# RWKV outputs of a two-block network: sums by accumulating transfers and head-by-head ScalarE steps for eight of ten tiles

## The reference, cut to what matters

```
rw_l = rw_l_f + flip_t(rw_l_b)
rw_c = rw_c_f + flip_t(rw_c_b)
...
mean = jnp.mean(rw_y, axis=-1, keepdims=True)
var = jnp.mean(jnp.square(rw_y - mean), axis=-1, keepdims=True)
gn = ((rw_y - mean) * lax.rsqrt(var + RWKV_GN_EPS)).reshape(bl, l, RWKV_W) * rw_ln_w + rw_ln_b
bonus = sum(jnp.sum(r * dirs[d][1] * rw_rk, axis=-1, keepdims=True) * v for d in range(2))
rw_o = (gn + bonus.reshape(bl, l, RWKV_W)) * jax.nn.silu(u[..., E_WZ:E_SHIFT])
```

## Time and profile before

| | |
|---|---|
| median of 3 runs | 4666.36 us (4665.85 to 4668.23) |
| profiled execution, its own time | 4666.31 us |
| span in the profile | 4664.5 us |
| PE busy | 4091.0 us (88%) |
| PE weight loads busy | 3356.1 us (72%) |
| DVE busy | 2628.1 us (56%) |
| ACT busy | 1482.7 us (32%) |
| POOL busy | 648.3 us (14%) |
| RWKV stage | about 2865 to 3500 us of the span |

### The profile page before, as it was taken

One profiled execution on the slowest core, in us unless ns is written; L12 is line 12 of the kernel. 1 busy time (PEld: TensorE's weight loads), 2 busy tenths in 40 slices (PEclk: granted clock), 3 DMA queues, 4 the chain that ended last, 5 costly groups with the idle time before them and its releaser, 6 DMA issues. The chain is left out here.

```text
span 4664.5 us, 74388 instructions
## 1 busy us (share of the span) xinstructions
PE 4091.0 (88%) x28926; PEld 3356.1 (72%) x28926; DVE 2628.1 (56%) x5018; ACT 1482.7 (32%) x3133; POOL 648.3 (14%) x860
## 2 busy tenths in 40 slices
PE   6999998867999989699996586899868899989988
PEld 5998887556888877599986233787757789955646
DVE  4567774666334348611227586777765335565746
ACT  4233321744222235311004243334434311143432
POOL 1111111000000000011123112000010024333320
PEclk8999999888999999799997688999878999999989
DMA  5544442542111145422323485444434335453334
GB/s 194 172 150 145 146 136 84 186 154 89 47 45 46 35 145 162 128 87 86 119 100 106 148 307 207 112 117 133 118 91 151 125 118 187 155 156 102 97 106 141
DMA packets 429678, 598.68 MB, mean 128 GB/s; under 512 B 168495, under 2 KB 317443, under 8 KB 426725
## 3 DMA queue, kind: packets, MB, share of 16 engines
q1 hardware_dynamic: 377069, 417.99, 29.6%
q0 software_dynamic: 50192, 173.75, 10.0%
q10 hardware_dynamic: 2088, 2.49, 0.2%
HBM read 429.40 MB, written 164.71 MB: 127 GB/s over the span
## 5 line engine op out<-in xcount | busy, mean ns | idle before, releaser
L612 PE MATMUL g_in_g_acc<-g_in_g_whi,g_in_hi 128*128 128x444 f32 (+4 forms) x960 | 357.2, 372 | 15.3 <-DVE g_in_g_wlo L600 10.3
L613 PE MATMUL g_in_g_acc<-g_in_g_wlo,g_in_hi 128*128 128x444 f32 (+4 forms) x960 | 346.4, 361 | 0.0
L614 PE MATMUL g_in_g_acc<-g_in_g_whi,g_in_lo 128*128 128x444 f32 (+4 forms) x960 | 345.7, 360 | 0.0
L612 PE MATMUL g_even_g_acc<-g_even_g_whi,h_hi 128*128 128x428 f32 (+2 forms) x800 | 289.8, 362 | 11.8 <-DVE g_even_g_wlo L600 11.8
L613 PE MATMUL g_even_g_acc<-g_even_g_wlo,h_hi 128*128 128x428 f32 (+2 forms) x800 | 289.3, 362 | 0.0
L614 PE MATMUL g_even_g_acc<-g_even_g_whi,h_lo 128*128 128x428 f32 (+2 forms) x800 | 289.3, 362 | 0.0
L612 PE MATMUL g_odd_g_acc<-g_odd_g_whi,h_hi 128*128 128x344 f32 (+3 forms) x816 | 263.7, 323 | 24.7 <-DVE g_odd_g_o L632 14.4
L5223 DVE SCALAR_TENSOR_TENSOR up_cv<-up_acc,up_taps,up_cv 128x1023 f32<-128x1023 f32 x88 | 112.8, 1282 | 281.4 <-ACT up_cv L5199 274.1
L614 PE MATMUL g_odd_g_acc<-g_odd_g_whi,h_lo 128*128 128x344 f32 (+3 forms) x816 | 262.0, 321 | 0.0
L613 PE MATMUL g_odd_g_acc<-g_odd_g_wlo,h_hi 128*128 128x344 f32 (+3 forms) x816 | 261.4, 320 | 0.0
L5178 PE MATMUL up_acc<-h_hi,up_w_hi 128*128 128x512 f32 x704 | 220.3, 395 | 8.7 <-DVE up_w_lo L5216 8.7
(11 more groups left out here) (585 smaller groups left out, 9741.4 us busy)
## 6 DMA issues: line engine op xcount, KB each, us to landing
down_raw<-in_w_down SPq DMA_DIRECT2D x66, 512.0 KB
g_in_m_w<-in_ada_w SPq DMA_DIRECT2D x24, 1024.0 KB, 5.6
up_w_buf<-in_w_up SPq DMA_DIRECT2D x44, 512.0 KB
g_odd_x<-U3p SPq DMA_DIRECT2D x24, 768.0 KB, 6.8
g_in_m_w<-in_w_ada SPq DMA_DIRECT2D x16, 1024.0 KB, 5.9
prep_near<-U2q SPq DMA_DIRECT2D x18, 896.0 KB
PD<-prep_od POOLq DMA_DIRECT2D x10, 1536.0 KB, 9.0
rwkv_xd<-PD SPq DMA_DIRECT2D x20, 768.0 KB
```

The lines of the kernel that those rows point to most:

```text
L612: pe.matmul(bank[:, :wd], hi[:, k, tt], w_hi[:, st % 2, k, :wd], start=k == 0, stop=False)
L613: pe.matmul(bank[:, :wd], hi[:, k, tt], w_lo[:, st % 2, k, :wd], start=False, stop=False)
L614: op = pe.matmul(bank[:, :wd], lo[:, k, tt], w_hi[:, st % 2, k, :wd], start=False, stop=k == KC - 1)
```

## The change

For outputs 0 to 7:

- The second direction is no longer loaded into `yo` and added by DVE. SP loads `RW[0]` into `yx` (new semaphore `y_half`), and a new POOL step `y_sum` waits for it and issues a transfer that adds `RW[1]` into `yx` (`accum_op`).
- `y_square` is eight activations of 64 columns, one for each head, with `accum_out` to `yvars`; the DVE sum of the squares goes away.
- The bonus leaves POOL: a new ACT step `y_gain`, between `y_silu` and `y_root`, multiplies v by the head's number in eight activations of 64 columns, scaled by a column of `ydots`. Then `s.y_bonus` rises.
- The row `rw_ln_b` is added into `yv` by a new POOL step `y_bias`, a second accumulating transfer with the row broadcast over partitions. `y_end` waits for its landing (`y_biased`).

Outputs 8 and 9 keep their code; their bonus on POOL signals `y_bonus_late`. `y_load_z` of 8 and 9 still waits for `s.y_bonus >= n - 1`. The first, replaced copies of the functions are gone from the file too; the instructions of all other stages stand as before.

```diff
-              ... ("T2_out", -1), ("y_silu", 1), ("y_root", 1), ("turn0", 2), ...
+              ... ("T2_out", -1), ("y_silu", 1), ("y_gain", 1), ("y_root", 1), ("turn0", 2), ...
-              ... ("y_scale", 1), ("X1", 0),
+              ... ("y_scale", 1), ("y_bias", 1), ("X1", 0), ("y_sum", 0),
...
-             ("y_silu", K8 - 1), ("y_root", K8 - 1), ("y_scale", K8 - 1), ("y_end", K8 - 1), ("u", END), ("u_out", END),
+             ("y_silu", K8 - 1), ("y_gain", K8 - 1), ("y_bias", K8 - 1), ("y_root", K8 - 1), ("y_scale", K8 - 1), ("y_end", K8 - 1), ("u", END), ("u_out", END),
...
-                    got = own_in[n] if n >= K8 else s.y_in
...
-                    sp.dma_start(yx[:, d], RW[0, tile, :]).then_inc(got, DMA)
-                    sp.dma_start(other_in(n), RW[1, tile, :]).then_inc(got, DMA)
+                    if n >= K8:
+                        sp.dma_start(yx[:, d], RW[0, tile, :]).then_inc(own_in[n], DMA)
+                        sp.dma_start(other_in(n), RW[1, tile, :]).then_inc(own_in[n], DMA)
+                    else:
+                        sp.dma_start(yx[:, d], RW[0, tile, :]).then_inc(s.y_half, DMA)
...
+                if what == "y_sum":
+                    pool.wait_ge(s.y_half, (n + 1) * DMA)
+                    pool.dma_start(yx[:, d], RW[1, i * P:(i + 1) * P, :], accum_op=ALU.add).then_inc(s.y_in, DMA)
+                if what == "y_bias":
+                    pool.wait_ge(s.y_bonus, n + 1)
+                    pool.dma_start(yv[:].rearrange("p h d -> p (h d)"), ln_b.partition_broadcast(P), accum_op=ALU.add).then_inc(s.y_biased, DMA)
-                if what == "y_bonus":
+                if what == "y_bonus" and n >= K8:
...
-                    act.activation(by_head(other_in(n)), yx[:, d].rearrange("p (h d) -> p h d", d=HD), ACT.Square).then_inc(s.y_squared, 1)
+                    if n >= K8:
+                        act.activation(by_head(other_in(n)), yx[:, d].rearrange("p (h d) -> p h d", d=HD), ACT.Square).then_inc(s.y_squared, 1)
+                    else:
+                        for h in range(HN):
+                            act.activation(yo[:, h * HD:(h + 1) * HD], yx[:, d, h * HD:(h + 1) * HD], ACT.Square, accum_out=yvars[:, d, h])
+                        act.drain()
+                        act.sem_inc(s.y_squared, 1)
+                if what == "y_gain":
+                    act.wait_ge(s.y_in_z, (n + 1) * (3 * DMA))
+                    for h in range(HN):
+                        act.activation(yv[:, h], yv[:, h], ACT.Copy, scale=ydots[:, d, h])
+                    act.drain()
+                    act.sem_inc(s.y_bonus, 1)
```

More of the change, by code:

```diff
@@ L29 @@
-ALPHA = 2.0 ** 0.25
-DMA = 16
-@contextmanager
-def stage(nc, name, *signals):
-    sems = {s: nc.alloc_semaphore(f"{name}_{s}") for s in signals}
-    with ExitStack() as mem:
-        def sb(label, shape, dt=F32):
-            return mem.enter_context(nc.sbuf_tensor(f"{name}_{label}", shape, dt))
-        def ps(label, shape=(P, 512), dt=F32):
-            return mem.enter_context(nc.psum_tensor(f"{name}_{label}", list(shape), dt))
-        with nc.Block() as block:
-            yield block, namedtuple("Signals", signals)(**sems), sb, ps
-    nc.clear_and_free_semaphores(list(sems.values()))
-    nc.all_engine_barrier()
@@ L3332, in part @@
                     pool.drain()
-                    pool.sem_inc(s.y_bonus, 1)
+                    pool.sem_inc(s.y_bonus_late, 1)
                 if what == "y_end":
@@ L3635, in part @@
                         dve.wait_ge(own_in[n], 2 * DMA)
[L3636 to L3639 removed]
+                        dve.tensor_tensor(yn, yn, other_in(n), ALU.add)
+                        dve.drain()
+                    else:
+                        dve.wait_ge(s.y_in, (n + 1) * DMA)
                     dve.tensor_reduce(ymean[:, :, 0], yn.rearrange("p (h d) -> p h d", d=HD), AX_X, ALU.add)
@@ L3657, in part @@
                     dve.tensor_tensor(yn, yn, yw[:, 0], ALU.mult)
-                    dve.wait_ge(s.y_bonus, n + 1)
+                    if n >= K8:
+                        dve.wait_ge(s.y_bonus_late, n - K8 + 1)
+                    else:
+                        dve.wait_ge(s.y_biased, (n + 1) * DMA)
                     dve.drain()
@@ L6327 @@
-BASE = 16
-NB = P // BASE
-LEVELS = (4, 5, 6)
-def rwkv_tables():
-    j, t = np.arange(P)[:, None], np.arange(P)[None, :]
-    sums = np.zeros((2, P, P), np.float32)
-    ends = np.zeros((2, P, 2), np.float32)
-    pairs = np.zeros((2, P, 4, P), np.uint32)
-    level = np.zeros((2, P, len(LEVELS) - 1, HD), np.float32)
-    own = (t % HD) + HD * (j // HD)
-    for d in range(2):
-        upto = (j <= t) if d == 0 else (j >= t)
-        before = (j < t) if d == 0 else (j > t)
-        mid = (j < 64) if d == 0 else (j >= 64)
-        sums[d] = upto.astype(np.float32) - mid
-        ends[d, :, 0], ends[d, :, 1] = 1.0 - mid[:, 0], mid[:, 0]
-        for n, m in enumerate((before, upto, before, upto)):
-            pairs[d, :, n] = m
-        for n, lv in enumerate(LEVELS[:-1]):
-            b = 1 << lv
-            same = (j // (2 * b)) == (own // (2 * b))
-            late = ((j // b) % 2) == (1 - d)
-            early = ((own // b) % 2) == d
-            level[d, :, n] = (same & late & early)[:, 0:HD]
-    eye = np.tile(np.eye(BASE, dtype=np.float32).reshape(1, BASE * BASE), (NB * HN, 1))
-    return sums, ends, pairs, level, eye
@@ L7160, in na_tables @@
-def na_tables():
-    q, k = np.arange(GRID_C)[:, None], np.arange(GRID_C)[None, :]
-    lo = np.clip(q - WIN_C // 2, 0, GRID_C - WIN_C)
-    inside = (k >= lo) & (k < lo + WIN_C)
-    hot = np.zeros((2 * WIN_C, GRID_C, GRID_C), np.float32)
-    for o in range(2 * WIN_C - 1):
-        hot[o] = inside & (k - q + WIN_C - 1 == o)
-    hot[2 * WIN_C - 1] = np.where(inside, 0.0, NEG)
-    return hot.reshape(2 * WIN_C, GRID_C * GRID_C)
-FWD_BLOCKS, CONV_BLOCKS = 4 * FCH, 8 * FCH
-TURN_FROM, PAIRS = 3, 9
@@ L7813 @@
-def kernel(**inputs):
-    import concourse.bacc as bacc
-    from concourse.bass_utils import run_bass_kernel_spmd
-    nc = bacc.Bacc("TRN2", target_bir_lowering=False, num_devices=1)
-    arrays, T = {}, {}
-    for name, a in list(inputs.items()) + list(tables().items()):
-        a = np.ascontiguousarray(a)
-        arrays[f"in_{name}"] = a
-        T[name] = nc.dram_tensor(f"in_{name}", a.shape, mybir.dt.from_np(a.dtype), kind="ExternalInput").ap()
-    T["out"] = nc.dram_tensor("out_y", (1, SEQ, D), F32, kind="ExternalOutput").ap()
-    program(nc, T)
-    r = run_bass_kernel_spmd(nc, [arrays], core_ids=[0])
-    return r.results[0]["out_y"]
```

3257 lines of the change are left out of this document (5 added, 3252 removed), and 7 rows, old and new, of the table PERIOD.

## The result

| | before | after |
|---|---|---|
| median of 11 runs each, on one chip | 4666.36 us (4657.14 to 4671.67) | 4678.32 us (4670.35 to 4687.87) |
| ratio after to before | | 1.0027, 95% interval 1.0018 to 1.0036 |
| span of the profiled execution | 4664.5 us | 4673.3 us |

The changed kernel takes 12.6 us more (0.0027 x 4666; 8.4 to 16.8 us by the interval). The forecast was 4674, 8.0 us more, with a range from 4662 to 4686. The profiled execution of the changed kernel was 3.0 us faster than its median (4675.37 for 4678.32), that of the kernel before was at its median.

What follows compares the result with a forecast made beforehand. No one engine bounds the RWKV stage; waits change hands between VectorE, TensorE and ScalarE. Terms -6.1 - 5.2 - 0.8 + 2.8 + 8.2 = -1.1 us, plus 9.1 at the end, +8.0 us: 4674 us, range 4662 to 4686.

Steps and rivals of the forecast that it cites:

- Addition off VectorE: Periods 10, 12 and 14 to 19, ahead of `weigh` or `keep`: eight additions of 0.76 us go, transfers hidden, -6.1 us.
- Stretched `weigh`: Ahead of `turn1`: `weigh` steps stretched beside GpSimd's bonus return to 0.69 us in four periods, -5.2 us.
- Squares and their sum: Periods 18 and 19: head-by-head squares ahead of `keep` cost +2.8 us; VectorE's dropped sum gives -0.8 us in period 18.
- Bonus on ScalarE: Between `T2_out` and arT: 2.05 us more makes `pairs0` start 1.6 us later in five periods, +8.2 us.
- The end: End of stage: output 9's load waits for output 7's `y_gain`, its bias transfer follows output 9's bonus, +9.1 us.
- TensorE cools in the new wait: Rival, ahead of `pairs0`: idle time in five periods costs TensorE's clock, 8 us more, 4682 us; chance 0.15.
- One slow stretch less: Rival: both periods with TensorE's clock at 0.80 come to 0.88, up to 3.3 us back each, 4669 us; chance 0.17.
- The adding transfers: Rival: they land so slowly, over some 15 us, that the centring waits; 4686 us at 17 us; chance 0.10.
- the other two: Rivals: ScalarE's gain hidden ahead of `pairs0`, 4659 or 4657 us, chance 0.08; the change not doing what it says, nothing.

Runs made afterwards that it cites:

- sum_only: The kernel before with only the second direction of the eight outputs brought by an adding transfer; squares whole, bonus on GpSimd: ratio 0.9992 to the kernel before.
- gain_late: The changed kernel with `y_gain` listed behind `u_out` instead of ahead of arT, nothing else: ratio 1.0000 to the kernel before.
- bonus_pool: The changed kernel with bonus and bias row of all eight outputs on GpSimd as before; adding transfer and squares head by head stay: ratio 0.9992 to the kernel before.
- best_bonus_pool: late_and_end with the bonus of all eight outputs on GpSimd: ratio 0.9971 to the kernel before.
- late_and_end: The changed kernel with `y_silu`, `y_gain`, `y_root` behind `u_out`, the stage's end reordered, output 7's bonus on GpSimd: ratios 0.9975 and 0.9966 to the kernel before.

## Why the prediction came out, point by point

The total came out; inside it one term was too small and the rest gave more than its terms, and that these nearly cancelled is luck. The forecast of +8.0 us lies just under the interval of the measured 12.6 us (8.4 to 16.8).

- **Addition off VectorE, -6.1 us.** The size fits: sum_only gives -3.7 us by time and -8.0 by the stretches. The place doesn't: all of it is in A, in the periods with a centring only, and more than half of it isn't the additions' own length. The transfers are hidden, as said: VectorE waits for none of the eight. They take 4.1 us from issue to landing (page rows below).
- **Stretched `weigh`, -5.2 us.** The rows are right: in the changed kernel every step of `weigh` is back at 0.69 us. The worth is supported by A alone, which is 4.9 us shorter in gain_late than in bonus_pool, and less by best_bonus_pool (2.3 and 3.8 us in A); in both the bonus on GpSimd stretches four steps, by some 3 us in all and not by 5.2.
- **Squares and their sum, +2.8 and -0.8 us.** The length is right: eight pairs from 3193.95 to 3195.97, 2.0 us. The worth is too small for these runs to show.
- **Bonus on ScalarE, +8.2 us.** Right in place and length (2.00 us), too small as a term. I had it as 1.6 us per period, since 0.4 us seemed to be off. TensorE's waits were 3.9, 3.9, 2.0, 2.3 and 2.1 us, and gain_late shows 11.7 us in A, with four of the periods, and 0.9 in B, with the fifth: 12.6 us. What failed in periods 11 and 13 is the use made of arT being 0.3 us early or late in the kernel before: true, but TensorE had come there at half clock. With the addition and the stretched steps gone it came early and at full clock, and then stood. In 15, 16 and 17 it still came at half clock, and the wait is the gain's own 2.0 us; what failed there is that the time behind the wait was put at nothing (`T0` 1.92 to 1.97 us for 1.15). The term's own bounds, -3 to +1.4, count four periods, where the sum has five and the end once more.
- **What hid this.** The rest of the change was worth more than its terms: gain_late less before is -11.1 us in A and B, where the terms other than `y_gain` add up to -9.3. The two errors (+4.4 and -1.8) left A and B at +1.5 us, where I had -1.1. The second is below what one profile tells.
- **The end, +9.1 us.** Right in every link, 1.3 us too much: the bonus of output 9 began 3.9 us after the load, not 4.3, the adding transfer was waited for 4.0 us from its issue (3481.75 to 3485.76), not 5.0, and it was issued 0.6 us behind GpSimd's last product, not at once. VectorE stood 7.7 us for it, not some 10.
- **The rivals.** "TensorE cools in the new wait" is nearer to the rows than the forecast: 2.9 us per period, where the forecast had 1.6 and this rival 3.2, at a chance of 0.15. Its sum, 16 us, is inside the measured interval. Its ground, that the clock follows TensorE's idle time in the period, is not borne out: period 11 has 5.7 us of idle at 0.94 in the changed kernel and 2.3 us at 0.88 in the kernel before. "One slow stretch less" happened too, but elsewhere than I had put it: the clock rose from 0.88 to 0.94, 0.95 and 1.00 in periods 11, 13 and 14, fell from 0.89 to 0.85 in 15 and stayed at 0.80 in 16. The adding transfers are not slow, and the other two didn't occur.
- **What stays open.** The timed difference is 12.6 us, the stage's 9.3 in one profile. The rest, 3.3 us, is inside the interval; the profiled execution was 3.0 us faster than its kernel's median. When TensorE's clock falls isn't settled either (last section).

## What to carry to other kernels

Before work is moved to an idle engine, look at what that engine's program has behind the new place, not at its busy share: the same 2.0 us of ScalarE cost 2.9 us per period ahead of the copy that TensorE waits for, and behind it no more than the stretched VectorE steps that they replace (late_and_end and best_bonus_pool agree within their intervals). A moved step also moves every semaphore that it raises; here one such rise, of one output of eight, held back a load by 4.6 us, and with the transfer listed behind that load's work it cost 7.4 us. And where an engine arrives late because its clock is low, "the operand was just in time" is no margin: take the stall ahead of it away and the operand is late. Last, profile the same kernel twice before a single period of it is explained.
